# An encoder's attention on one Trainium2 core: P V in two passes with V's two parts side by side, a written order of a head per engine, and the sums of exponentials spread through memory

## The reference, cut to what matters

```python
def one_block(args):
    qn_b, qr_b = args
    sc = (einsum('bqhd,bkhd->bhqk', qn_b, k_nope) + einsum('bqhr,bkr->bhqk', qr_b, k_rope))
    w = jax.nn.softmax(sc * scale, axis=-1)
    return jnp.einsum('bhqk,bkhd->bqhd', w.astype(v.dtype), v)
...
mix = jnp.concatenate([group_rms_norm(attn, g_attn_out[i], N_HEADS),
                       group_rms_norm(conv, g_conv_out[i], CONV_GROUPS)], axis=-1)
x = x + rms_norm(mix @ w_out[i], g_post_mix[i])
```

## Time and profile before

| | |
|---|---|
| median of 3 runs | 2934.0 us |
| the profiled execution | 2934.37 us, of which its span is 2932.6 us |
| PE busy | 2860.4 us (98%) |
| DVE, ACT, POOL busy | 1689.9, 1194.0, 112.0 us |
| instructions | 35106 |

### The profile page before, as it was taken

How to read it: one execution, slowest core, us unless ns; L and a number is a source line. 1 busy time by engine, 2 the same in 40 slices (tenths; PEclk the granted TensorE clock), 3 DMA queues, 4 the chain that set the end, 5 groups by cost and what they waited for, 6 DMA issues and landing times.

```text
span 2932.6 us, 35106 instructions
## 1 busy us (share of the span) xinstructions
PE 2860.4 (98%) x13696; PEld 2376.5 (81%) x13696; DVE 1689.9 (58%) x2232; ACT 1194.0 (41%) x1793; POOL 112.0 (4%) x78
## 2 busy tenths in 40 slices
PE   6998999999999999999999999999999999999996
PEld 5877888888888888888887788887888888888885
DVE  4356667556444444468765567773654544544786
ACT  4335676545111121226643367664532211212473
POOL 0221000000000000000013200000000000000000
PEclk9999999999999999999999999999999999999998
DMA  4120000432111111112232100006211111111232
GB/s 146 58 76 34 22 23 20 155 133 76 43 43 57 43 43 57 43 64 97 98 112 73 48 28 24 24 15 240 73 50 51 54 46 43 57 43 43 72 101 72
DMA packets 61002, 190.69 MB, mean 65 GB/s; under 512 B 6752, under 2 KB 6752, under 8 KB 60896
## 3 DMA queue, kind: packets, MB, share of 16 engines
q1 hardware_dynamic: 60896, 189.22, 19.3%
HBM read 164.03 MB, written 25.17 MB: 65 GB/s over the span
## 4 chain that ended last, share of the span: by engine, by line
PE 94%; DVE 3%; ACT 1%; DMA 1%; POOL 1%; issue 0%; SPq 0%; DVEq 0%; ACTq 0%
PE ps L753 29%; PE ps L755 29%; PE ps L754 29%; PE ps L924 4%; PE ps L959 1%; DVE ptl L1773 1%; PE ps L799 0%; PE ps L821 0%; PE ps L792 0%; PE ps L885 0%; ACT pth L1187 0%; DVE hl L1557 0%; DVE wl L1557 0%; POOL cv L1968 0%; DMA raw<-w_units 0%
## 5 line engine op out<-in xcount | busy, mean ns | idle before, releaser
L753 PE MATMUL ps<-hh,wh 128*128 128x512 f32 x2192 | 871.4, 398 | 30.2 <-DVE wl L1557 23.4
L754 PE MATMUL ps<-hl,wh 128*128 128x512 f32 x2192 | 856.7, 391 | 0.0
L755 PE MATMUL ps<-hh,wl 128*128 128x512 f32 x2192 | 856.3, 391 | 0.0
L753 PEld LDWEIGHTS ps<-hh,wh 128*128 128x128 f32 x2192 | 413.5, 189 | 125.5 <-issue 26.8
L754 PEld LDWEIGHTS ps<-hl,wh 128*128 128x128 f32 x2192 | 413.8, 189 | 93.5 <-issue 8.2
L755 PEld LDWEIGHTS ps<-hh,wl 128*128 128x128 f32 x2192 | 413.5, 189 | 86.8
L1187 ACT ACTIVATE wh<-raw 128x1024 fp32r<-128x1024 f32 x244 | 254.8, 1055 | 381.2 <-PE ps L755 369.8
L753 PE MATMUL ps<-gh,wh 128*128 128x512 f32 x1024 | 398.6, 389 | 0.0
L755 PE MATMUL ps<-gh,wl 128*128 128x512 f32 x1024 | 398.4, 389 | 0.0
L754 PE MATMUL ps<-gl,wh 128*128 128x512 f32 x1024 | 398.3, 389 | 0.0
L1895 DVE TENSOR_TENSOR xf<-xf,ps 128x512 f32<-128x512 f32 x464 | 310.9, 684 | 146.1 <-PE ps L755 145.5
(11 more groups left out here) (134 smaller groups left out, 3233.7 us busy)
## 6 DMA issues: line engine op xcount, KB each, us to landing
raw<-w_units SPq DMA_DIRECT2D x240, 512.0 KB, 3.5
hh<-mix_hi SPq DMA_DIRECT2D x16, 512.0 KB, 6.1
hl<-mix_lo SPq DMA_DIRECT2D x16, 512.0 KB, 7.0
stage<-w_head SPq DMA_DIRECT2D x16, 320.0 KB, 3.1
xf<-x_in SPq DMA_DIRECT2D x4, 1024.0 KB, 8.8
mix_hi<-cyh SPq DMA_DIRECT2D x8, 512.0 KB, 2.7
mix_lo<-cyl SPq DMA_DIRECT2D x8, 512.0 KB, 3.6
mix_hi<-yh SPq DMA_DIRECT2D x32, 128.0 KB, 2.2
```

The source lines that it names most:

```text
L753: nc.tensor.matmul(dst, ah, bh, start=start, stop=False)
L754: nc.tensor.matmul(dst, ah, bl, start=False, stop=False)
L755: return nc.tensor.matmul(dst, al, bh, start=False, stop=stop)
```

## The change

Six things change, all in the attention stage.

1. `vh` and `vl` become one tensor `vv`, by parity of the head: for each chunk 64 columns of zeros, 64 of V's high part, 64 of its low part. `values` now has two matmuls for a chunk: `[high | low]` by `pth`, and `[zeros | high]` by `ptl`. One half of the output rows holds high times high, the other low times high plus high times low. DVE adds the halves (`output_sum`, one 64x512 operation more for each half of a head).
2. The sums of exponentials no longer come from PE. The Exp on ACT also gives the sum along its row (`accum_out`), in `den`, one column for a step.
3. These sums are squared and spread: POOL squares 4 columns (128x4), DVE turns them to rows (`V.transpose`, 128x32), SP stores four rows of 32 for each of four parts into the memory tensor `sums` (4 DMAs) and loads one row of 512 back to all 64 rows of the other half of `sq` (1 DMA). `variances` waits for that load.
4. ACT copies one half of the bank to `of`, DVE adds, and only then ACT squares (64x512 where it was 128x512).
5. The loops `head(...)` are replaced by one written sequence of a head per engine (`ATT_PE`, `ATT_ACT`, `ATT_DVE`), walked by `attend(h)` for h = 0 to 8. `name.o.args`: o is the head relative to h.
6. SP's queue has another order, with the stores and loads of the sums in it.

```diff
+ATT_PE = steps("""
+turn.0.0.0 turn.0.0.1 score.0.2 kv.1.0 score.0.3 turn.0.1.0 turn.0.1.1 kv.1.1 pv.-1.3.0 pv.-1.3.1 turn.0.2.0
...
+ATT_ACT = steps("""
...
+high.0.6.1 last.1 square.0.0 high.0.7.0 high.0.7.1 exp.1.0 ln.0.0 r.0.0 last.2 last.3
+""")
...
+                def store_sums(h, t):
+                    O = (L * HEADS + h) * 2 + t
+                    sp.wait_ge(den_turn, O + 1)
+                    for b in range(4):
+                        sp.dma_start(sums[O].rearrange("(s b i) -> b s i", s=4, b=4)[b],
+                                     dent[32 * b:32 * b + 4, t, :]).then_inc(den_out, 16)
+                def load_sums(h, t):
+                    O = (L * HEADS + h) * 2 + t
+                    sp.wait_ge(den_out, 64 * O + 64)
+                    if O:
+                        sp.wait_ge(o_ln, O)
+                    sp.dma_start(sq[rows(1 - h % 2), 0, :], sums[O:O + 1].partition_broadcast(V_DIM)).then_inc(den_in, 16)
...
+                for h in range(HEADS):
+                    if h:
+                        store_attention((h - 1) // 2, (h - 1) % 2, 0)
+                    store_sums(h, 0)
+                    load_sums(h, 0)
+                    if h + 3 < HEADS:
+                        load_head(h + 3)
+                    if h + 1 < HEADS:
+                        store_sums(h, 1)
+                        load_sums(h, 1)
+                        if h:
+                            store_attention((h - 1) // 2, (h - 1) % 2, 1)
...
                 for c in (4, 7, 0, 1, 2):
                     load_mix(c, mix_in)
+                store_sums(HEADS - 1, 1)
                 store_attention(PAIRS - 1, 0, 1)
+                load_sums(HEADS - 1, 1)
...
                     for c in range(4 * part, 4 * part + 4):
-                        last = split_product(dst, vh[:, c, a * V_DIM:a * V_DIM + P], vl[:, c, a * V_DIM:a * V_DIM + P],
-                                             pth[:, G % 2, c, :], ptl[:, G % 2, c, :], c == 0, c == 7)
+                        nc.tensor.matmul(dst, vv[:, a, c, V_DIM:3 * V_DIM], pth[:, G % 2, c, :], start=c == 0, stop=False)
+                        last = nc.tensor.matmul(dst, vv[:, a, c, 0:2 * V_DIM], ptl[:, G % 2, c, :], start=False, stop=c == 7)
...
                 def variances(h, a, t):
-                    pe.wait_ge(o_copy, (L * HEADS + h) * 2 + t + 1)
+                    O = (L * HEADS + h) * 2 + t
+                    pe.wait_ge(o_sq, O + 1)
+                    pe.wait_ge(den_in, 16 * O + 16)
...
                 def exponentials(h, s):
-                    act.wait_ge(s_least, step(L, h, s) + 1)
+                    S = step(L, h, s)
+                    act.wait_ge(s_least, S + 1)
+                    if h or s >= 2:
+                        act.wait_ge(t_out, 2 * S - 2)
...
-                                         ACT.Exp, bias=nm[:, s % 2:s % 2 + 1], scale=-1.0).then_inc(s_exp, 1)
+                                         ACT.Exp, bias=nm[:, s % 2:s % 2 + 1], scale=-1.0,
+                                         accum_out=den[:, h % 2, s:s + 1]).then_inc(s_exp, 1)
...
+                def output_sum(h, a, t):
+                    dve.wait_ge(o_copy, (L * HEADS + h) * 2 + t + 1)
+                    V.tensor_tensor(of[rows(a), :], of[rows(a), :], ps[rows(a), 6 + t, :], ALU.add).then_inc(o_sum, 1)
```

More of the change, by code:

```diff
@@ L225, with head_steps @@
 """)
+def head_steps(h, order):
+    for kind, ahead, *more in order:
+        if kind == "last":
+            if h == HEADS - 1:
+                yield kind, h, ahead
+        elif 0 <= h + ahead < HEADS:
+            if not (kind in ("score", "exp", "least") and h + ahead == h + 1 == HEADS):
+                yield (kind, h + ahead, *more)
 STATS_AT = {
@@ L452, in encoder @@
         lr_lo = sem("lr_lo")
-        v_ones = sem("v_ones")
+        v_zero = sem("v_zero")
         kv_out = sem("kv_out")
@@ L910, in scores, with transposes @@
                     last.then_inc(s_out, 1)
-                def transposes(h, s, first, piece):
+                def transposes(h, s, b):
                     S = step(L, h, s)
                     pe.wait_ge(s_exp, S + 1)
[L916 to L926, removed]
@@ L928, in bank_free @@
-                def bank_free(h, s, first):
-                    H = L * HEADS + h
-                    if s == 0:
-                        if first:
-                            pe.wait_ge(q_f, H * 2 + 2)
+                    if h or s:
+                        pe.wait_ge(t_lo, 2 * S + b - 1)
+                    else:
+                        pe.wait_ge(cv_ln, L * 8 + 8)
+                    if s == 4 and b == 1 and h + 1 < HEADS:
+                        pe.wait_ge(v_lo, L * HEADS + h + 2)
+                    for c in range(4):
+                        last = nc.tensor.transpose(ps[:, 4 + b, c * P:(c + 1) * P],
+                                                   pr[:, s % 2, (4 * b + c) * P:(4 * b + c + 1) * P], ident)
@@ L938, in bank_free @@
[L938 to L948, removed]
+                    if (G, part) == (2, 0):
+                        if h + 1 < HEADS:
+                            pe.wait_ge(q_f, H * 2 + 4)
+                        else:
+                            pe.wait_ge(o_ln, H * 2)
@@ L1444, in _ @@
                 exponentials(0, 0)
[L1445 to L1455 removed]
+                for h in range(HEADS + 1):
+                    attend(h)
                 def steps_of(order):
@@ new lines, in attend @@
+                def attend(h):
+                    for kind, o, *n in head_steps(h, ATT_DVE):
+                        a = o % 2
+                        if kind == "low":
+                            low_of_transposed(o, *n)
+                        elif kind == "least":
+                            minima(o, *n)
+                        elif kind == "k":
+                            keys_and_values(o, a, n[0], 6)
+                        elif kind == "v_turned":
+                            values_by_token(o, a, 0, 5)
+                        elif kind == "q":
+                            queries(o, a, n[0], 7)
+                        elif kind == "q_low":
+                            low_of_queries(o, a, n[0])
+                        elif kind == "den":
+                            turned_sums(o, n[0])
+                        elif kind == "sum":
+                            output_sum(o, a, n[0])
+                        elif kind == "scale":
+                            output(o, a, n[0], o // 2)
+                        elif kind == "y":
+                            low_of_output(o, a, n[0])
+                        elif kind == "unit" and o + 2 < HEADS:
+                            split_head(L, o + 2, a)
+                        elif kind == "last":
+                            split_unit(L, O_AT + n[0])
```

338 lines of the change are left out of this document (159 added, 179 removed).

## The result

The changed kernel takes 2898.92 us (median; 2898.12 to 2900.16), the kernel before 2934.24 (2932.72 to 2935.05): a ratio of 0.9881 with an interval of 0.9863 to 0.9898. The forecast was 2898. The profiled execution took 2898.12 with a span of 2896.3, against a span of 2932.6 before: 36.3 us less.

A forecast was written before the change was run, and what follows sets the result against it. PE, busy 98%, was taken to bound the kernel. From 2934.4 us, terms of -51.6 (pass), +2.4 (SP waits), +1.4 (head 0), +10.2 (stage end) and +1.7 (clock) gave 2898.5, in medians 2898; range 2886 to 2907.

The forecast's parts named there:

- The pass: P V on PE: 512 matmuls fewer at 0.119 us, 61.2 us of PE's stream, 51.6 of it ahead of head 7.
- Rival D: P V: two matmuls cost as much as three because the weight load sets the pace, no gain, 2930; chance 0.03.
- The heads: Mid-stage attention: a head falls from 39.12 to 35.3 us, with PE running through and ACT and DVE keeping up.
- waits for SP: Heads 2 to 7: ACT's yh waits for a late output store, 0.2 us a head, 2.4 us in all.
- 1 us of room: Within a head: ACT can wait about 1 us for the late output store before DVE and PE are held up.
- rival C: Every head: the output store stands behind the sums' landing; a landing of 8 us gives 2960, slower; chance 0.05.
- Head 0: Start of each layer's attention: no earlier P V as cover, 0.7 us of waits a layer, 1.4 in all.
- The sum in the Exp: ACT: the row sum adds 0.14 us to each Exp, 1.1 us a head, and ACT doesn't become the bound.
- The end of the stage: Last head: sums and weight units land later, last variances move from T0 + 38.9 to 44.0, 5.1 us a layer, 10.2 in both.
- Rival A: End of the stage costs nothing net and the heads run through: 2873 to 2883 us; chance 0.14.
- The clock: PE at 0.50 of the clock after its wait at the first layer's end: 1.7 us, added once.
- a landing of 4.8 us: Sums' small stores, read and written back, landing in twice the usual time: 2 us lost a head, 2922, in case B.

The follow-up runs named there:

- e3: The changed kernel with a third matmul of the same shape put back into each chunk of P V: 2951.55 us, ratio 1.0057.
- e5: The kernel before with V's low pass left out of P V, its old order, stores and sums kept: 2886.5 us, ratio 0.9827.
- e4: The changed kernel without the stores and loads of the sums through memory and without the waits for them: 2892.24 us, ratio 0.9853.
- e7: The changed kernel with SP waiting for the second sums to land before it stores the output half of the head before: 2920.41 us, ratio 0.9948.
- e10: The changed kernel with yl of the second half written sooner on DVE and its output store ahead of the second sums on SP: 2894.75 us, ratio 0.9865.
- e6: The changed kernel with the row sum taken out of the Exp and ones in the sums' place: 2896.66 us, ratio 0.9863.
- e8: The changed kernel with head 7's ten loads and weight units issued earlier, output stores ahead of second sums, unit copies spread over head 7: 2878.03 us, ratio 0.9801.
- e9: As e8, with yl written sooner on DVE and the ten loads cut in three pieces around head 7's first sums: 2871.37 us, ratio 0.9788.
- e1: The changed kernel with the projection's third and fourth weight units loaded ahead of head 7's second sums and output store: 2893.04 us, ratio 0.9858.

## Why the prediction was right, and where it wasn't

**The pass.** 512 matmuls at 0.119 us held, 0.121 in e3: e3 shows it from the one side, e5 from the other. Rival D (two matmuls cost as much as three) is out. Whether the weight load or the columns set the 0.119 us isn't told apart, since each of these matmuls has both.

**The heads.** Forecast 35.3 and 2.4 us of waits for SP. Measured 35.05 and 3.5 us of waits (2.2 in layer 1, 1.4 in layer 2, against 210.3 for six heads without the trip in e4). The two errors go against each other. The first: I took the old head less 32 matmuls, but the old order kept PE waiting and the new one doesn't; with three passes this is 0.19 us a head (39.11 against 38.92 in e3), with two 0.5 (35.55 in e5 against 35.05). The second: I gave ACT 1 us of room for a late store. In heads 2 to 6 of layer 1 ACT waited 0.68, 1.06, 1.33, 0.37 and 0.53 us for it and the heads grew by 0.40, 0.50, 1.05, 0 and 0.25, so the room was about 0.3 to 0.6. That it is the store, through `yh`, `k`'s low part and PE, is shown by e7, which lengthens it, and by e10, which takes it away with the trip left in place.

Why the store is as late as forecast is luck. I had the load of the second sums wait 2.4 us for their landing, and the store behind it. In head 3 the load is indeed issued 2.5 us after the four stores of the sums:

```profile
395.98 1.25 SPq L736 DMA_DIRECT2D sums<-dent  x4
399.73 0.47 SPq L745 DMA_DIRECT2D sq<-sums  x1
400.24 0.60 SPq L728 DMA_DIRECT2D mix_hi<-yh  x1
400.88 1.69 SPq L728 DMA_DIRECT2D mix_lo<-yl  x1
```

But the landing isn't what it waits for. `load_sums` also waits for `o_ln`, the Ln of the half before, which comes behind the `variances` that read the place in `sq` that the load overwrites. ACT's timeline has this Ln end at 399.65, 0.08 us ahead of the load, and shows the wait that follows:

```profile
399.06 0.59 ACT L1447 ACTIVATE sq<-ps 64x512 f32<-64x512 f32 x1
...
404.43 0.63 ACT L1234 ACTIVATE yh<-of 64x512 fp32r<-64x512 f32 x1 [1.33 <-DMA mix_lo<-yl]
```

The `variances` were done at 397.98, so a wait for them in place of Ln would let the load go sooner; the store would still wait for `yl`, written at 399.45. No run tries it. In the second sums of each of heads 1 to 6 in both layers the load goes 0.06 to 0.08 us behind the end of Ln, 2.1 to 2.5 us behind the four stores. The first sums of a head, where Ln is done before, have their load 0.9 us behind the stores. So the sums' landing costs the heads nothing, and a landing longer by about 1.2 us would still cost nothing: rival C named the wrong gate, though e7 shows that its chain behind a late store is right. A second thing isn't in my count either: four of the twelve pairs of stores have one half that takes 1.5 to 2 us to issue (1.69 here) where the others take 0.45 to 0.60, and these four have 5.0 of the 8.4 us that ACT waits for stores. Why some issues are so long stays open.

**Head 0.** 34.4 and 34.2 us in the two layers: -5.5 instead of -4.3. I had put 0.7 us a layer of waits there; PE is busy for 34.31 of 34.39, so there are hardly any.

**The sum in the Exp.** 0.20 us, not 0.14, as an instruction of its own, and the turn on DVE 0.20, not 0.15; e6 finds 2.3 us for the sum in the Exp, not clear of noise, and neither engine became the bound.

**The end of the stage.** The size was right (5.7 and 5.4 against 5.1), and so were the places, with errors that cancelled. The ten loads started at T0 + 15.8, not 16.9, because the sums' first trip was quicker: the four issues took 1.26 us, where I had taken 1.8, and from their end (520.91) to the load's issue at 521.79 are 0.88 us, where I had taken 2.4 for landing. They landed by about 537.9 (the last was issued at 527.28, and the longest landing of L763's loads from 522 to 528 us is 10.6), T0 + 31.3 and not 33.0. I said that the second sums would land with the ten loads and the units be issued only then: 538.68 is that, 3.0 us behind the four stores, here with Ln long over (535.48). What the step left out is the second gate, the output store behind the late `yl`, which holds the queue to T0 + 30.8 by itself. That failed in e4's expectation, which took the trip as the only gate and was 7 us too low. The units then took 4.0 to 4.7 to land, not 3.5 to 3.9, and PE waited 9.50 and 7.51 us, not 7:

```profile
551.17 2.08 PE L1011 MATMUL ps<-sq,cst 128*128 128x512 f32 x2 [9.50 <-ACT sq L1440]
```

ACT's timeline shows the chain of those us, the two units' copies first:

```profile
543.16 1.06 ACT L1234 ACTIVATE wh<-raw 128x1024 fp32r<-128x1024 f32 x1 [7.01 <-DMA raw<-w_units]
544.57 1.06 ACT L1234 ACTIVATE wh<-raw 128x1024 fp32r<-128x1024 f32 x1 [0.36 <-DMA raw<-w_units]
547.70 0.63 ACT L1234 ACTIVATE yh<-of 64x512 fp32r<-64x512 f32 x1 [2.07 <-DVE of L1843]
549.14 0.59 ACT L1234 ACTIVATE of<-ps 64x512 f32<-64x512 f32 x1 [0.81 <-DVE yl L1613]
550.49 0.63 ACT L1440 ACTIVATE sq<-of 64x512 f32<-64x512 f32 x1 [0.76 <-DVE of L1838]
```

The last half's copy, sum and square need nothing from the units; they stand behind them in ACT's order. That is why units for which ACT waits 7 us make `variances` late, and why e8 and e9 take the unit copies out of that place. Rival A (the end costs nothing) is what e9 reaches, not what the change does.

**The clock.** Windows inside the waits of layers 1 and 2, 5 us each:

```profile
545.00:550.00 5.00, 0.00 (x0) 0.00 (x0) 3.37 (x5) 1.84 (x3) 0.00 (x0) 0.50 1.01 413
...
1965.00:1970.00 5.00, 0.00 (x0) 0.00 (x0) 3.53 (x5) 1.94 (x3) 0.00 (x0) 0.73 1.03 420
```

PE does nothing in either and the granted clock falls to 0.50, the 1.2 GHz level (0.73 is the mean of a window in which it falls). It is still 0.50 from 551.17 to 554.17 in layer 1, so the matmuls there run at half pace: two of `variances` take 2.08 us. From `variances` of layer 1 to layer 2's head 0 it is 1.5 us more than before, near the 1.7 forecast. In layer 2 the kernel before had its low stretch too, and no time is added. In e9, without the wait, the clock is 1.00 there.

**Not forecast: the start.** Head 0 of layer 1 starts at 259.71, 2.3 us later than before, though the change touches nothing ahead of it. Over the ten experiments, whose code there is that of the change or of the kernel before, it lies between 256.85 and 259.56, with one profile of each. The windows show where it arises, here the change and then e8, each from 50 to 60 us:

```profile
50.00:60.00 10.00, 10.00 (x32) 8.00 (x33) 10.00 (x15) 9.08 (x14) 0.00 (x0) 0.71 0.37 118
50.00:60.00 10.00, 10.00 (x41) 8.16 (x40) 10.00 (x15) 7.45 (x12) 0.00 (x0) 0.89 0.32 110
```

PE is busy throughout in both, but at a mean clock of 0.71 it gets through 9 matmuls fewer than at 0.89, 2.05 us at 0.228 each. e8 has the code of the change there and starts head 0 at 256.85; the kernel before has 0.89 too, while e5, with its code, has 0.71 and starts at 259.56. Both clocks occur with both codes, so this isn't the change's doing; why the clock differs there from profile to profile stays open. Without it the kernel would have come out 2.7 us below the forecast. That the forecast is within 0.4 us in the spans is thus luck; its parts are good to 1 or 2 us.

By the Trainium skill ("DMA: Bandwidth & Descriptors", Specifications) stores in pieces below 512 bytes are read and written back, which I had weighed as a landing of 4.8 us for the sums. No such price shows: their first trip took 0.88 us from the end of the last issue, and at the end of the stage, beside large loads, 2.4 to 3.0 (4.9 in e1, with the two units in flight as well). The same page ("Latency and other measured facts") gives about 800 ns as the least round trip to memory; the trace agrees with it: 0.88 us from the end of the last issue is the order of the shortest trip here.

## What to carry to other kernels

A pass taken from the engine that is busy 98% counted in full in mid-stage, and the pace of its matmuls is read from distances on the timeline, not from their mean. Whatever is added to a queue in strict order is paid at the stage's end, where loads for the next stage stand behind it: list everything ahead of the load that is needed first, since with two gates in a row the removal of either alone shows almost nothing. List for each load all that it waits for, too: the load of the second sums seemed to wait for their landing and waited for an Ln. And where work for the next stage stands ahead of the last piece of this one in an engine's order, its transfer is on the critical path. Moving these, the loads and the stores together (e9) was worth 27.5 us, against 35.3 for the change itself.

## What the runs showed of the hardware that was not expected

- The sum of an activation's output costs ACT a row of its own: 198 ns for 128x1, beside an Exp of 1024 columns that stays at 1114 ns.
- A small store's price depends on what is in flight: four stores of 4 x 128 bytes each had landed 0.88 us after the last left the queue when it was quiet, and 2.4 to 3.0 us after it behind ten loads of 512 KB.
- Waits of ACT for a store are partly covered: in e7 it waited 12.4 us for `mix_lo<-yl` between 300 and 500 us, and PE behind it 9.0.
